# The overflow blocks of a routed expert stage: 32 instead of 33 blocks ahead of the branch

## The chip, the cores and the metric

The kernel runs on one core of a Trainium2 chip. The time is that of the device for one execution, in microseconds (us); smaller is better. The engines are TensorE (PE, with PEld for its weight loads), VectorE (DVE), ScalarE (ACT), GpSimd (POOL) and SyncE (SP), and 16 DMA engines move data between HBM and the on-chip memory.

## The reference

Two blocks of a model run one after the other on 512 tokens of width 1024, in f32. The first block has two layers; each is an attention part, a hierarchical mixture of experts, and a gated embedding. The change touches only the mixture of experts, which runs once in each of the two layers:

```python
expert_id = (g_sel[:, None] * EXPERTS_PER_GROUP + top_i).reshape(-1)   # 2 of 32 experts for each token
counts = jnp.zeros((N_EXPERTS,), jnp.int32).at[expert_id].add(1)
...
def expert_block(args):
    xb, e = args
    hid = jax.nn.silu(xb @ w_gate[e]) * (xb @ w_up[e])
    return hid @ w_down[e]
```

The 512 tokens give 1024 assignments, 32 for an expert in the mean. One expert has three matrices of 1024 x 256, 1024 x 256 and 256 x 1024 in f32, 1 MiB each. The inputs are drawn from a fixed seed, so the counts are the same in every run.

## The kernel before

Each layer runs attention, then merge_and_route (L1375: projections, router, and the tables that say which token sits where), then the experts, then combine_experts (L1914: reads the experts' rows back from HBM, weighs them and adds them to the tokens), then the gate of the embedding.

**The blocks.** The kernel puts assignments into blocks of LANES = 64 rows (L1336). Expert e owns block e, for its first 64 assignments. What an expert has beyond 64 goes to overflow blocks, 32 and up; there can be at most SPILL = 16 of them, so BLOCKS = 48. L1634 to L1647 count them on VectorE: `spills` is the number of overflow blocks of each expert, `ends` its running sum. Three tables come out: r.token (which token each lane gathers; two blocks are one column), r.row (which half row of y_rows each lane scatters to), and r.spill_expert (L1667 to L1670), whose entry j is the expert of overflow block j, at most 31, and whose entry 16 is the number of overflow blocks. For an entry past the last overflow block the value is 31, the cap. An empty lane has an index out of bounds, and the indirect DMA leaves it out.

**experts (L1702)** runs `blocks` blocks from block `first`. Its five engines work as a pipeline:

- SyncE (L1734 to L1751) loads the three matrices of each block into one of U slots, in order. Gate and up of block n wait until block n-U has had its product with gate and up (gu_done), down waits for down_done of block n-U. For a block of 32 or more the expert's number is read from r.spill_expert into a register first (value_load, L1737); nothing in the loads depends on whether the block holds any token. At the end it loads two halves of w_ple, the embedding's weights, into the two gather buffers (L1748).
- GpSimd (L1754) gathers the token rows of a pair of blocks (L1758) and scatters the 64 x 1024 result of each block, as 128 half rows (L1765). At the end it waits for the scatters (L1781).
- TensorE (L1784) turns the rows of a pair (turn, L1789), multiplies with gate and up (L1800), turns the hidden (L1809), multiplies with down (L1818). Block n-1's down runs after block n's gate and up.
- ScalarE applies silu (L1849) and evicts the result (L1844); VectorE scales the turned rows (L1864), multiplies (L1873) and copies (L1879).

It is called in two ways. With `opening`, the call "ex": U is 6 slots, the first 6 blocks' weights and the first 2 pairs' rows were loaded during routing (L1438 to L1445, L1467), and at its end TensorE and ScalarE do the first 4 pieces of the embedding's product (L1835, L1904, L1911). Without it, the call "sp": U is EMBED_SLOT = 3 slots, nothing has been loaded ahead, GpSimd first clears the two gather buffers (L1773), and SyncE waits at its end for the reload of w_ple (L1750), whose place the gathers have taken.

Every such call is a Block: each engine runs its own code, and all five meet at its end. The two calls stand in first_layer:

```python
spilled = nc.values_load(r.spill_expert[0:1, SPILL:SPILL + 1], min_val=0, max_val=SPILL)
experts(k, "ex", r, i, 0, ALWAYS, ...)            # ALWAYS = EXPERTS + 1 = 33
with nc.If(spilled > ALWAYS - EXPERTS):
    experts(k, "sp", r, i, EXPERTS, SPILL, ...)   # 16 blocks from block 32
```

So block 32, the first overflow block, is run by the first call always, and the second call runs all 16 overflow blocks, the first of them again, when there are two or more of them.

Of the kernel before, what the change touches and what calls it, by code (L numbers as in the profile page):

```python
# [75 lines left out]
def sems(k, ctx, names):  # L76

    found = [ctx.enter_context(k.nc.semaphore(n + k.layer)) for n in names.split()]
    assert not k.used_sems & {x.num for x in found}
    k.used_sems |= {x.num for x in found}  # L80
    return found
# [143 lines left out]
def row_piece(w, c, chunks, off, cols):  # L225

    return [(chunks, cols, rows_pc(w)[:, c:c + chunks, off:off + cols])]
# [1106 lines left out]
EXPERTS = GROUPS * PER_GROUP  # L1334
# [1 line left out]
LANES = P // 2  # L1336
SPILL = 2 * S // LANES
BLOCKS = EXPERTS + SPILL
ALWAYS = EXPERTS + 1
SKIP = 65536.0  # L1340


# [352 lines left out]
def expert_parts(k, u, w_gate, w_up, w_down):  # L1695

    gu, down = expert_slot(k, u)
    return [(gu[:, 0, :], w_gate.rearrange("(p c) n -> p (c n)", c=DC)),
            (gu[:, 1, :], w_up.rearrange("(p c) n -> p (c n)", c=DC)), (down, w_down.rearrange("(f p) n -> p f n", p=P))]
# [214 lines left out]
def combine_experts(k, tag, r, y_rows, embedding, st):  # L1914


    nc = k.nc
    rows = y_rows.rearrange("(t p c) d -> p t (c d)", p=P, c=2)
    y = k.expert_ring[:, 0:NT * 2 * D].rearrange("p (t c d) -> p t c d", t=NT, c=2)
    with ExitStack() as ctx:  # L1920
        (*landed, added, multiplied) = sems(k, ctx, " ".join(f"{tag}_landed{t}" for t in range(NT)) + f" {tag}_added {tag}_multiplied")
        block = ctx.enter_context(nc.Block())

        @block.sync
        def _(sp):
            for t in range(NT):
                sp.dma_start(y[:, t, :, :].rearrange("p c d -> p (c d)"), rows[:, t, :]).then_inc(landed[t], 16)
            st.loads(sp, 0, st.RAW)

        @block.gpsimd  # L1930
        def _(pool):
            st.split_highs(pool, 0, st.SPLIT)

        @block.tensor
        def _(pe):
            for i in range(NT, 2 * NT):
                embedding.product(i, k.ps[:, i % NT, :]).then_inc(multiplied, 1)

        @block.scalar
        def _(act):  # L1940
            for i in range(NT, 2 * NT):
                act.wait_ge(multiplied, i - NT + 1)
                embedding.take(i, k.ps[:, i % NT, :])
            act.preload_act_table_set("sqrt_and_others")

        @block.vector
        def _(dve):
            for t in range(NT):
                dve.wait_ge(landed[t], 16)
                for c in (0, 1):  # L1950
                    nc.vector.scalar_tensor_tensor(out=k.x[:, t, :], in0=y[:, t, c, :], scalar=r.gate[:, c, t:t + 1],
                                                   in1=k.x[:, t, :], op0=ALU.mult, op1=ALU.add).then_inc(added, 1)
                    dve.wait_ge(added, 2 * t + c + 1)
# [1195 lines left out]
def first_layer(k, t, i, ctx, following, r, ring_base, scratch, o, line_store):  # L3149


    nc = k.nc
    xn_rows, y_rows = scratch
    st = o.st
    lasting = {x.num for x in st.landed + [st.high_ready, st.low_ready, st.used]}
    ended = k.used_sems - lasting
    early = k.spare[:, 0:6 * S].rearrange("p (j s) -> p j s", j=6)
    route_loads = r.loads(k, ctx, t["w_router_group"][i], t["b_router_group"][i], t["w_router_expert"][i],
                          t["b_router_expert"][i], t["g_ffn"][i])
    k.room(o.branches, "yb_room", [P, 8 * S])  # L3160
    with ExitStack() as room:
        attention, yb_ready, early_ready = differential(
            k, ctx, room, st, [t[n][i] for n in ("lam_q1", "lam_k1", "lam_q2", "lam_k2")], t["g_subln"][i],
            t["c_lam_init"][i], t["c_keep"][i], k.cosT, k.sinT, o.da_raw, o.ybT, early,
            line_store)
    o.branches.close()
    assert -(-nc.sbuf_base // 32) * 32 == ring_base
    mergedT = k.spare.rearrange("p (c s) -> p c s", c=DC)
    m = Merge(k, ctx, "mg", st, MERGE_PIECES, o.packs, ((o.yaT, 4), (o.ybT, 4)), mergedT, o.sig, o.part,
              (0, 1, 2, 3, 4, 7, 5, 6), early, early_ready)  # L3170
    op = Product(k, ctx, "op", st, m.end, DC, mergedT, o.split)
    with ExitStack() as room, ExitStack() as moe:
        k.expert_ring = k.room(room, "expert_ring", [P, RING_SLOTS * EXPERT_WORDS])
        xs = k.room(room, "ex_xs", [P, GATHERS, D])
        embedded = k.spare_tiles
        embedding = Embedding(k, moe, "pe", t["p"][i, 0], t["w_ple"][i], o.rows, embedded)
        embedding.weights_in(xs)
        weights = (t["w_exp_gate"], t["w_exp_up"], t["w_exp_down"])
        expert_loads = Loads(k, moe, *((f"ex_{n}_landed{u}", expert_parts(k, u, *(w[i, u] for w in weights))[part])
                                       for u in range(EXPERT_SLOTS)  # L3180
                                       for n, part in (("gu", slice(0, 2)), ("down", slice(2, 3)))))
        gathered = sems(k, moe, " ".join(f"ex_gathered{u}" for u in range(GATHERS)))
        lasting = {x.num for x in expert_loads.landed + gathered + embedding.loads.landed + [embedding.ready]}
        merge_and_route(k, "rt", st, attention, yb_ready, m, op, r, xn_rows, route_loads, expert_loads, embedding, xs, gathered,
                        ended)
        ended = k.used_sems - lasting
        ctx.close()
        spilled = nc.values_load(r.spill_expert[0:1, SPILL:SPILL + 1], min_val=0, max_val=SPILL)
        experts(k, "ex", r, i, 0, ALWAYS, xn_rows, y_rows, *weights, xs, embedding, (expert_loads, gathered), ended)
        with nc.If(spilled > ALWAYS - EXPERTS):  # L3190
            experts(k, "sp", r, i, EXPERTS, SPILL, xn_rows, y_rows, *weights, xs, embedding)
        before_gate = set(k.used_sems)
        raw = k.expert_ring[:, 2 * NT * D:3 * NT * D].rearrange("p (t d) -> p t d", t=NT)
        gate_stream = Stream(k, following, "pg", [row_piece(t["w_ple_gate"][i], 2 * e, 2, half * 512, 512) for half in (0, 1)
                                            for e in range(4)], raw, ring_base + 4 * 3 * NT * D)
        lasting = k.used_sems - before_gate
        combine_experts(k, "cb", r, y_rows, embedding, gate_stream)
    ended = k.used_sems - lasting

    def ple(ctx, late, sig, junk, following):  # L3200
        return embed_per_layer(k, ctx, "pe", gate_stream, t["g_ple"][i], embedded, sig, junk, late, following, ended), gate_stream

    return ple
# [132 lines left out]
```

## Time and profile before

| | |
|---|---|
| median of 3 runs | 2538.68 us (2536.31 to 2541.02) |
| the profiled execution's own time | 2538.29 us |
| its span (first to last instruction) | 2536.5 us |
| mean granted TensorE clock | 0.966 |
| TensorE busy | 2319.1 us (91%) |
| VectorE, ScalarE, GpSimd busy | 998.9, 586.7, 411.4 us |
| moved by DMA | 402.85 MB, mean 159 GB/s |

A busy time is the sum over one engine's instructions; waits between them are not in it. The span is cut into 40 slices of 63.4 us. The mixture of experts runs from about 482 to 737 us in the first layer and from about 1275 to 1532 us in the second. In the timeline a row has its start, its length, the engine and line, output and inputs, the count of instructions merged into it, and in brackets how long the engine was idle before it and what ended that. SPq is SyncE's issue of a DMA: its length is the issue, not the transfer.

### The profile page before, as it was taken

The numbers are of one execution on the slowest core, as the hardware profiler recorded it, in microseconds if no ns is written. First come the engines' busy times: TensorE is split into PE (matmuls) and PEld (weight loads), VectorE is DVE, ScalarE is ACT, GpSimd is POOL, SyncE is SP. The second block draws the span as 40 slices with busy tenths as digits, with TensorE's granted clock in tenths as the row PEclk, the third lists the DMA queues.
The fourth block names the chain that finished last, engine by engine and source line by source line (L and its number), as shares of the span: only waits on it lengthen the run. The fifth ranks groups of instructions, "written<-read, shape, count | busy, mean of one in ns | idle before, by whom it ended". The sixth has DMA issues, their size and how long they took to land. (4 is left out here: it accounts for less than half of the span.)

```text
span 2536.5 us, 29194 instructions
## 1 busy us (share of the span) xinstructions
PE 2319.1 (91%) x11776; PEld 1707.9 (67%) x11776; DVE 998.9 (39%) x1730; ACT 586.7 (23%) x1211; POOL 411.4 (16%) x404
## 2 busy tenths in 40 slices
PE   7989999698879999999779887899999999999998
PEld 5666788444437766788644445787767887888886
DVE  5445533511125454543521113645553334332234
ACT  2433401211113352420311112423432001200011
POOL 2001121121211101021112211111111211111111
PEclk9999999799989999999889998899999999999999
DMA  4114535799962212233789995222222333233321
GB/s 147 51 50 99 131 105 199 277 414 415 416 253 92 67 34 65 60 91 100 290 342 416 415 367 178 67 83 68 80 84 65 98 96 108 83 93 99 100 91 67
DMA packets 291540, 402.85 MB, mean 159 GB/s; under 512 B 31306, under 2 KB 230730, under 8 KB 273478
## 3 DMA queue, kind: packets, MB, share of 16 engines
q1 hardware_dynamic: 276444, 373.31, 41.7%
q0 software_dynamic: 10176, 16.81, 1.8%
q10 hardware_dynamic: 4778, 10.76, 1.6%
q8 instruction: 98, 1.61, 0.3%
q14 instruction: 44, 0.36, 0.0%
HBM read 388.99 MB, written 30.15 MB: 165 GB/s over the span
## 5 line engine op out<-in xcount | busy, mean ns | idle before, releaser
L136 PE MATMUL banks<-h_split,w_high 128*128 128x512 f32 x2624 | 830.5, 398 | 2.3 <-PEq L3022 1.7
L136 PEld LDWEIGHTS banks<-h_split,w_high 128*128 128x128 f32 x2624 | 482.2, 189 | 108.1 <-issue 8.2
L188 DVE TENSOR_TENSOR w_low<-w_raw,w_high 128x1024 fp32r<-128x1024 f32 (+1 forms) x264 | 316.9, 1202 | 528.4 <-POOL w_high L177 528.4
L177 POOL CAST w_high<-w_raw 128x1024 fp32r<-128x1024 f32 (+1 forms) x264 | 278.4, 1056 | 1474.6 <-PE banks L136 1351.7
L136 PE MATMUL banks<-h_split,w_low 128*128 128x512 f32 x1312 | 515.1, 393 | 0.0
L136 PEld LDWEIGHTS banks<-h_split,w_low 128*128 128x128 f32 x1312 | 246.8, 188 | 55.2
L136 PE MATMUL banks<-w_high,op_split 128*128 128x512 f32 x736 | 231.2, 394 | 0.9 <-DVE mg_part L1264 0.9
L1800 PE MATMUL banks<-expert_ring,ex_xsT 128*64 128x256 f32 x1472 | 176.4, 394 | 12.3 <-DMA expert_ring<-in_w_exp_up 9.3
L136 PEld LDWEIGHTS banks<-w_high,op_split 128*128 128x128 f32 x736 | 138.2, 188 | 34.0 <-DVE mg_part L1264 2.2
L1800 PEld LDWEIGHTS banks<-expert_ring,ex_xsT 128*64 128x64 f32 x1472 | 105.6, 141 | 68.7 <-DMA expert_ring<-in_w_exp_up 10.3
L136 PE MATMUL banks<-w_low,op_split 128*128 128x512 f32 x368 | 144.7, 393 | 0.0
L1765 POOL DMA_INDIRECT y_rows<-ex_y,route_row x66 | 65.8, 997 | 388.8 <-ACT ex_y L1844 388.8
L136 PE MATMUL banks<-w_high,h_split 128*128 128x512 f32 (+1 forms) x384 | 120.0, 387 | 2.7 <-DVE h_split L336 2.5
L1873 DVE TENSOR_TENSOR ex_hid<-ex_silu,banks 128x128 f32<-128x128 f32 x66 | 19.0, 288 | 261.6 <-ACT ex_silu L1849 261.6
L1248 ACT ACTIVATE mg_sig<-banks 128x512 f32<-128x512 f32 x44 | 26.4, 599 | 347.2 <-PE banks L136 347.2
L1818 PE MATMUL banks<-expert_ring,ex_hidT 128*64 128x512 f32 x368 | 96.0, 646 | 0.9 <-issue 0.9
L1789 PE MATMUL banks<-identity,ex_xs 128*128 128x128 f32 x272 | 42.1, 301 | 58.5 <-DMA ex_xs<-xn_rows,route_token 42.2
L136 PE MATMUL banks<-pg_high,h_split 128*128 128x512 f32 x256 | 85.1, 408 | 2.5 <-DVE h_split L336 2.5
L136 PEld LDWEIGHTS banks<-w_high,h_split 128*128 128x128 f32 x384 | 72.0, 192 | 17.9 <-DVE h_split L336 3.7
L1789 PEld LDWEIGHTS banks<-identity,ex_xs 128*128 128x128 f32 x272 | 34.8, 196 | 72.8 <-DMA ex_xs<-xn_rows,route_token 53.6
L1844 ACT ACTIVATE ex_y<-banks 128x512 f32<-128x512 f32 x66 | 39.5, 598 | 189.6 <-PE banks L1818 189.6
L136 PEld LDWEIGHTS banks<-w_low,op_split 128*128 128x128 f32 x368 | 69.1, 188 | 16.0
(422 smaller groups left out, 2782.2 us busy)
## 6 DMA issues: line engine op xcount, KB each, us to landing
w_raw<-in_w_in SPq DMA_DIRECT2D x142, 512.0 KB, 4.1
expert_ring<-in_w_exp_gate SPq DMA_DIRECT2D x46, 1024.0 KB
expert_ring<-in_w_exp_up SPq DMA_DIRECT2D x46, 1024.0 KB
expert_ring<-in_w_exp_down SPq DMA_DIRECT2D x46, 1024.0 KB
w_raw<-in_w_gu SPq DMA_DIRECT2D x44, 512.0 KB, 4.1
region<-in_w_exp_gate SPq DMA_DIRECT2D x20, 1024.0 KB
region<-in_w_exp_up SPq DMA_DIRECT2D x20, 1024.0 KB
region<-in_w_exp_down SPq DMA_DIRECT2D x20, 1024.0 KB
```

Of the source, the lines that this page charges most:

```text
L136: last = nc.tensor.matmul(out, left, right, start=(start and n == 0), stop=(stop and n == 2), skip_group_check=True)
L177: self.nc.gpsimd.tensor_copy(self.high[:, i % self.SPLIT, 0:n], self.raw[:, i % self.RAW, 0:n]).then_inc(self.high_ready, 1)
L188: self.nc.vector.tensor_tensor(self.low[:, i % self.SPLIT, 0:n], self.raw[:, i % self.RAW, 0:n], self.high[:, i % self.SPLIT, 0:n].bitcast ...
L1248: self.nc.scalar.activation(out, gate, ACT.Sigmoid).then_inc(self.sig_done, 1)
L1765: nc.gpsimd.indirect_dma_start(out=y_halves, in_=y[:, n % Y, :], in_offset=None, out_offset=bass.IndirectOffsetOnAxis(ap=r.row[:, at:at + ...
L1789: last = nc.tensor.transpose(k.ps[:, c // 4, (c % 4) * P:(c % 4 + 1) * P], xs[:, q % X, c::DC], k.ident[:])
L1800: last = nc.tensor.matmul(k.ps[LANES * h:LANES * (h + 1), 2 + side, 0:2 * P].rearrange("p (g n) -> p g n", g=2), xsT[:, q % X, c, LANES * ...
L1818: last = nc.tensor.matmul(k.ps[LANES * h:LANES * (h + 1), 5 + n % 2, :], hidT[:, n % 2, LANES * f:LANES * (f + 1)], slots[n % U][1][:, f, ...
L1844: nc.scalar.activation(y[:, n % Y, :], k.ps[:, 5 + n % 2, :], ACT.Copy).then_inc(sem["y_ready"], 1)
L1873: nc.vector.tensor_tensor(hid[:, n % 2, :], silu[:, n % 2, :], k.ps[:, 2 + n % 2, P:2 * P], ALU.mult).then_inc(sem["hid_ready"], 1)
```

## The change

ALWAYS is gone. The first call runs the 32 blocks of the experts, and the branch is taken when there is one overflow block or more; taken, it runs the 16 blocks from block 32, as before.

```diff
-ALWAYS = EXPERTS + 1
...
         spilled = nc.values_load(r.spill_expert[0:1, SPILL:SPILL + 1], min_val=0, max_val=SPILL)
-        experts(k, "ex", r, i, 0, ALWAYS, xn_rows, y_rows, *weights, xs, embedding, (expert_loads, gathered), ended)
-        with nc.If(spilled > ALWAYS - EXPERTS):
+        experts(k, "ex", r, i, 0, EXPERTS, xn_rows, y_rows, *weights, xs, embedding, (expert_loads, gathered), ended)
+        with nc.If(spilled > 0):
             experts(k, "sp", r, i, EXPERTS, SPILL, xn_rows, y_rows, *weights, xs, embedding)
```

## Rows read from the trace of the kernel before

**Rows 1.** The page: the span, and GB/s moved in 40 slices of it.
```profile
span 2536.5 us, 29194 instructions
...
GB/s 147 51 50 99 131 105 199 277 414 415 416 253 92 67 34 65 60 91 100 290 342 416 415 367 178 67 83 68 80 84 65 98 96 108 83 93 99 100 91 67
```

**Rows 2.** A group of the page: out<-in, xcount, busy us, mean ns, idle before.
```profile
L1765 POOL DMA_INDIRECT y_rows<-ex_y,route_row x66 | 65.8, 997 | 388.8 <-ACT ex_y L1844 388.8
```

**Rows 3.** Windows: window, length, busy us (count) by engine, PEclk, DMA share, GB/s.
```profile
600.00:690.00 90.00, 77.00 (x524) 40.07 (x526) 14.71 (x36) 10.26 (x24) 18.26 (x18) 0.95 1.02 416
...
728.10:729.10 1.00, 1.00 (x4) 0.40 (x3) 0.00 (x0) 0.53 (x1) 0.00 (x0) 1.00 0.43 160
730.60:731.60 1.00, 1.00 (x4) 0.41 (x3) 0.00 (x0) 0.48 (x1) 0.00 (x0) 1.00 0.05 5
1526.30:1527.30 1.00, 1.00 (x4) 0.48 (x3) 0.00 (x0) 0.41 (x1) 0.00 (x0) 1.00 0.04 1
737.00:738.00 1.00, 0.00 (x0) 0.00 (x0) 0.00 (x0) 0.00 (x0) 0.00 (x0) 1.00 0.14 41
```

**Rows 4.** DMA view, window 730.6 to 731.6 us.
```profile
DMA packets 80, 0.00 MB, mean 5 GB/s; under 512 B 78, under 2 KB 78, under 8 KB 80
```

**Rows 5.** DMA view, window 1526.3 to 1527.3 us.
```profile
DMA packets 80, 0.00 MB, mean 1 GB/s; under 512 B 80, under 2 KB 80, under 8 KB 80
```

**Rows 6.** Timeline 700 to 745 us: start, length, engine, line, operation.
```profile
704.47 5.36 PE L1800 MATMUL banks<-expert_ring,ex_xsT 128*64 128x256 f32 x32 [2.63 <-DMA expert_ring<-in_w_exp_up]
...
712.98 3.67 PE L1800 MATMUL banks<-expert_ring,ex_xsT 128*64 128x256 f32 x32
...
720.51 3.67 PE L1800 MATMUL banks<-expert_ring,ex_xsT 128*64 128x256 f32 x32 [1.89 <-DMA expert_ring<-in_w_exp_up]
...
728.46 7.13 PE L1904 MATMUL banks<-ex_xs,pe_rows 128*128 128x512 f32 x16
...
729.44 0.98 POOL L1765 DMA_INDIRECT y_rows<-ex_y,route_row  x1 [1.63 <-ACT ex_y L1844]
...
735.63 0.60 ACT L1911 ACTIVATE region<-banks 128x512 f32<-128x512 f32 x1 [1.12 <-PE banks L1904]
...
737.03 2.87 SPq L1927 DMA_DIRECT2D expert_ring<-y_rows  x4
...
740.00 8.54 PE L1904 MATMUL banks<-ex_xs,pe_rows 128*128 128x512 f32 x16 [4.41 <-issue]
```

**Rows 7.** Timeline, the same place of the second layer.
```profile
1508.44 3.67 PE L1800 MATMUL banks<-expert_ring,ex_xsT 128*64 128x256 f32 x32
...
1516.14 3.67 PE L1800 MATMUL banks<-expert_ring,ex_xsT 128*64 128x256 f32 x32 [2.06 <-DMA expert_ring<-in_w_exp_up]
```

**Rows 8.** Timeline of SyncE's DMA issues, first layer, expert loads.
```profile
599.73 4.17 SPq L1742 DMA_DIRECT2D expert_ring<-in_w_exp_gate  x1
...
684.78 3.05 SPq L1742 DMA_DIRECT2D expert_ring<-in_w_exp_gate  x1
...
688.91 4.70 SPq L1744 DMA_DIRECT2D expert_ring<-in_w_exp_down  x1
...
694.41 2.02 SPq L1742 DMA_DIRECT2D expert_ring<-in_w_exp_gate  x1
```

**Rows 9.** Timeline 535 to 575 us, first layer, the pieces of a block.
```profile
541.92 1.00 POOL L1765 DMA_INDIRECT y_rows<-ex_y,route_row  x1 [3.23 <-ACT ex_y L1844]
...
545.57 1.16 PE L1789 MATMUL banks<-identity,ex_xs 128*128 128x128 f32 x8 [0.70 <-DMA ex_xs<-xn_rows,route_token]
...
546.65 1.94 PE L1818 MATMUL banks<-expert_ring,ex_hidT 128*64 128x512 f32 x8
...
568.82 1.00 POOL L1765 DMA_INDIRECT y_rows<-ex_y,route_row  x1 [3.23 <-ACT ex_y L1844]
```

**Rows 10.** Tile view of ex_xs on GpSimd: lengths in ns, min/median/max.
```profile
L1460 POOL MEMSET ex_xs<- x4: 948/952/953, 445.7 to 1240.8; 128x1024 f32 x4
```

**Rows 11.** DMA issues of the page: KB each, median us to landing.
```profile
ex_xs<-xn_rows,route_token POOLq DMA_INDIRECT x34, 8.4
```

## The prediction

> **What bounds the kernel now.** I read the page first, for where memory matters. TensorE is busy for most of the span, yet the change touches only the two expert stages, and there the slices move 414 to 416 GB/s, far more than anywhere else [rows 1]. The windows say more: from 600 to 690 us the DMA share is 1.02 at 416 GB/s, with TensorE busy 77.0 of 90 us [rows 3]. So an expert block is paced by its weights: 3 matrices of 1,048,576 bytes are 3.146 MB, and 3.146 / 415.5 GB/s is 7.57 us. With its gathers and scatters a block takes longer: ten blocks between two issues of a gate matrix, (684.78 - 599.73) / 10 = 8.5 us [rows 8]. TensorE alone could go faster. Early in the stage, when six slots are still full, four blocks pass between two scatters in 568.82 - 541.92 = 26.9 us, 6.73 each [rows 9]. At the end of the stage the reader should see that block 32's first product waits for DMA (1.89 us before 720.51), and block 31's, at 712.98, does not [rows 6].
>
> **Is there an overflow block?** This decides everything, because the branch is entered at one instead of two. All 66 scatters of the trace are 33 blocks in two layers, so the branch was never entered: neither layer has more than one overflow block [rows 2]. What block 32 held can be read from its scatter, the last of each layer. First a gauge: in the us after block 31's scatter in layer 0, 160 KB move, which is 39 rows of 4 KB [rows 3]; the reference's own routing of these inputs, counted, gives expert 31 39 tokens. Block 32 in layer 0 moves 5 KB, and of its 80 packets 78 are under 512 B; the two others are of 2 KB class, and a row is scattered as two halves of 2 KB [rows 3, 4]. So layer 0 has one overflow row. In layer 1 the same scatter moves 1 KB, and all 80 packets are under 512 B: no row [rows 3, 5]. The count of the reference agrees: in layer 0 one expert has 65 tokens, one above the 64 of its block, and in layer 1 the largest has 54. The number of overflow blocks is 1 in layer 0 and 0 in layer 1. With the change the branch is entered in layer 0, for one row, and not in layer 1.
>
> **What goes: block 32 of the first call, in both layers.** Its weights, its half pair's turn (1.16 us), its products. In layer 0 the stage's last gate product starts at 712.98 instead of 720.51: 7.53 us [rows 6]. It could gain a little more: a turn of 1.16 us stood ahead of it [rows 9] and goes, but block 31's matrices land about 7.57 us before block 32's, at 712.9, so I take 7.6. The bounds are 7.5 and 8.7. In layer 1: 1516.14 - 1508.44 = 7.70 [rows 7]. The loads of w_ple are issued behind the last block's weights and move up with them. Behind the last down product the tail is the same (four pieces of embedding, barrier). Sum 15.3 us saved.
>
> **What comes: 16 blocks in layer 0.** The branch has no case for one block; it runs SPILL blocks, each with its 3.146 MB. Blocks 33 to 47 are empty, and their entries of r.spill_expert are all 31, so they load expert 31's matrices fifteen times; nothing skips a load. Step by step, from the moment at which the second call may start:
>
> 1. The first call ends 7.6 us earlier, so SyncE, which issued the next stage's first DMA at 737.03 [rows 6], is at the branch at 729.4.
> 2. It reads the expert's number. Before block 32's gate matrix that made a gap of 694.41 - (688.91 + 4.70) = 0.80 us [rows 8]. First issue at 730.2.
> 3. A first DMA after a pause: y_rows is issued at 737.03 and in the us from 737 41 GB/s move [rows 3, 6], so data flow less than 1 us later. I take 1.0: 731.2.
> 4. The last block's gate and up are in after 15 and two thirds blocks: 15.67 x 7.57 = 118.6 us. Its first product starts at 849.8. No gathers to speak of run beside these loads (one row in all), so I take 7.57, not 8.5.
> 5. The tail. From block 32's gate product to its scatter it was 729.44 - 720.51 = 8.93 us, and the scatter's packets were through by 731.6 [rows 3, 6]: 11.1 us. The embedding's four pieces (7.13 us from 728.46) aren't run again. The barrier: from ScalarE's last end, 735.63 + 0.60, to 737.03 is 0.80 [rows 6]. So the next stage's first issue falls at 849.8 + 11.1 + 0.8 = 861.7.
>
> Against 737.03 that is +124.7 us for layer 0, its saved block already inside.
>
> Is anything else slower than the 7.57? **GpSimd's start:** two memsets of 0.95 us [rows 10], a gather at about 1 us of issue, 8.4 us to landing in the median under load [rows 11], turn and scale: TensorE may start its first product some 6 us after the matrices are in. That is hidden as long as DMA has work, and three free slots are 22.7 us of it. Block 3's down then waits for down_done of block 0, which comes behind block 1's gate product; I work it out to about 27 us after the start, when block 3's gate and up are still arriving (until 27.7). Cover is thin: 0 to 3 us. I take 0. **Three slots instead of six:** from the landing of block n's gate and up to the moment DMA needs down_done of n-1 there are two blocks, 15.1 us; TensorE needs 3.67 for gate and up, 1.16 for a turn and 1.94 for down [rows 6, 9]. Enough. **SyncE:** queued behind each wait for a slot is the read of a register (0.80) and three issues; they run while DMA is two blocks behind. Hidden. **w_ple:** 1.05 MB again, 2.5 us behind the last down matrix, while TensorE is in the 11.1 us tail. Hidden. It would cost its 2.5 us only if the tail were gone.
>
> **The jump.** Before, both layers jumped over the branch's code. TensorE resumed at 740.00, idle 4.41 us, while SyncE issued at 737.03 [rows 6]: 3 us that nobody waited for, since VectorE waited for y_rows. Whether entering the branch costs such a stall the trace can't show. Bounds: below, nothing or a small gain, since layer 0 now runs straight on; above, 4.4 us on SyncE. I take 0, because SyncE's own jump is the nearest row and shows 0.80 with the barrier in it. The Trainium skill (Runtime: NRT & Kernel Launch, section "Instruction fetch mechanics") says that a taken branch to code outside the fetched window stops the engine until that code is in, and calls run-time control flow expensive. By that rule an entered branch could stall SyncE too, and the sum would be about 4 us higher; the trace agrees for TensorE's 4.41 us and not for SyncE's 0.80.
>
> The pace itself: the same skill (DMA: Bandwidth & Descriptors, section "Where 436 GB/s comes from") says that between HBM and the on-chip memory HBM's 358 GB/s per core binds. By it the 16 blocks would take an estimated 19 us more. This trace differs, with its 416 GB/s held over 90 us on one core [rows 3], and the row decides.
>
> **Sum.** +124.7 - 7.7 = +117.0 on the profiled execution's own 2538.29 us, which stands 0.39 us below the median of the three runs: 2655.3 us.
>
> **The rivals.**
>
> - *TensorE paces the branch.* It wakes slowly after a wait for weights: behind 2.63 us idle a gate product took 5.36 instead of 3.67 us [rows 6]. If each block of the branch paid that, TensorE's 6.73 would become 8.42 us and pass DMA's 7.57: 16 x 0.85 = 13.6 us more, 2669. For it: with three slots every block waits a bit. Against it: a wait of 1.89 us still gave 3.67, and the idle time of a block would be 7.57 - 6.73 = 0.84 on the average.
> - *Faster than before: the branch is not entered in layer 0.* The place is the count of overflow blocks in `ends`, the price is 124.7 + 7.6 us, and it turns at one row: with no expert above 64 tokens only the two saved blocks are left, 2538.3 - 15.3 = 2523. For it only that two packets of 2 KB are a thin sign; against it, they are there in layer 0 and not in layer 1, and the reference's count says 65.
> - *Entered in both layers*, if the one row were read wrongly and block 32 held something in layer 1: 2538.3 + 2 x 124.7 = 2788. Rows 5 are against it.
>
> **How the numbers follow.** Forecast 0.84, TensorE's pace 0.11, not entered 0.03, entered twice 0.02. The range: the low end takes the lower pace bound in part (TensorE's 6.73 if reading one expert's matrices over and over let DMA go faster would give 13.6 less, and I give it little) and the larger saving of 8.7: 2645. The high end holds the first rival's 2669, the stall of 4.4 us and the late first slots, 3: 2676. That leaves out the two last rivals, 0.05, and part of the doubt on prices. A change of 0.2%, 5 us, is what a measurement of this kernel can tell from none; no case lies within it. Faster 0.03, slower 0.97.
>
> **What would show each step.** The scatter group has 64 + 16 = 80 instead of 66; DMA moves 16 - 2 = 14 blocks more, 44 MB, about 447 MB in all; the expert slices at 415 GB/s are two longer in layer 0 and none in layer 1. The gap from the last gate product of the branch to y_rows is near 12 us, from SyncE's first load to that product near 120. A pace of 8.4 us with products of 5.36 us would say TensorE; idle SyncE at the entry would say the jump. A scatter count of 64 would make the prediction wrong altogether.

## The result, and the profile after

| | before | after |
|---|---|---|
| median | 2539.85 us (4 runs, 2536.31 to 2544.76) | 2659.25 us (4 runs, 2656.23 to 2662.21) |
| the profiled execution | 2538.29 us | 2656.23 us |
| span | 2536.5 us | 2654.4 us |
| mean granted clock | 0.966 | 0.965 |

The ratio of after to before is 1.0466, with a 95% interval of 1.0449 to 1.0483: the kernel got 4.7% slower. The prediction was 2655.3 us with a range of 2645 to 2676, and the profiled execution stands 0.9 us from it, the median of the four runs 4.0 us above it. The sections below show that this closeness is partly luck: the terms for the first layer's branch fell short by 5 us, and stretches that no term spoke of gave 7.6 back.

The page of the changed kernel, with the lines that answer to [rows 1]:

```profile
span 2654.4 us, 30783 instructions
...
GB/s 142 54 50 110 121 96 254 326 414 415 318 397 379 159 80 40 58 53 88 81 299 345 416 416 274 144 96 80 85 73 56 96 93 111 80 95 97 102 93 67
...
DMA packets 301655, 448.01 MB, mean 169 GB/s; under 512 B 33994, under 2 KB 233418, under 8 KB 280006
```

The slices at more than 300 GB/s go on longer in the first layer, and the bytes are 448.01 MB against 402.85. The difference, 45.2 MB, is 14.4 times 3.146 MB: 16 blocks more, two fewer, and w_ple once more. The view of the scatters' line (columns as in [rows 10]) answers to [rows 2]:

```profile
L1764 POOL DMA_INDIRECT y_rows<-ex_y,route_row x64: 982/992/1020, 499.7 to 1644.2; - x64
...
L1764 POOL DMA_INDIRECT y_rows<-sp_y,route_row x16: 982/992/1023, 755.7 to 863.2; - x16
```

64 scatters of the first call and 16 of the branch, all 16 of them between 755.7 and 863.2 us. So the branch ran once, in the first layer, for the one row beyond an expert's 64, and not in the second. The timeline of the first layer, answering to [rows 6]:

```profile
714.08 3.67 PE L1799 MATMUL banks<-expert_ring,ex_xsT 128*64 128x256 f32 x32 [2.44 <-DMA expert_ring<-in_w_exp_up]
...
729.20 0.60 ACT L1910 ACTIVATE region<-banks 128x512 f32<-128x512 f32 x1 [1.12 <-PE banks L1903]
...
730.93 0.36 SPq L1741 DMA_DIRECT2D expert_ring<-in_w_exp_gate  x1
...
742.48 5.74 PE L1799 MATMUL banks<-expert_ring,sp_xsT 128*64 128x256 f32 x32 [1.47 <-DVE sp_xsT L1863]
...
762.41 3.67 PE L1799 MATMUL banks<-expert_ring,sp_xsT 128*64 128x256 f32 x32 [0.60 <-DMA expert_ring<-in_w_exp_up]
...
854.30 3.67 PE L1799 MATMUL banks<-expert_ring,sp_xsT 128*64 128x256 f32 x32 [1.99 <-DMA expert_ring<-in_w_exp_up]
...
863.22 0.98 POOL L1764 DMA_INDIRECT y_rows<-sp_y,route_row  x1 [1.63 <-ACT sp_y L1843]
...
867.73 2.01 SPq L1926 DMA_DIRECT2D expert_ring<-y_rows  x4
```

Block 31's gate product is now the last of the first call. SyncE's first load of the branch, 730.93, comes 1.1 us after ScalarE's last end (729.20 + 0.60). TensorE starts at 742.48, 11.6 us later, since it needs the gathered rows; from block 35 of the branch (762.41) on it waits for weights; and after the last scatter 4.5 us pass until the next stage's first issue at 867.73. The windows (columns as in [rows 3]) show DMA in the same stretch:

```profile
731.00:732.00 1.00, 0.00 (x0) 0.00 (x0) 0.00 (x0) 0.00 (x0) 0.73 (x2) 1.00 0.29 33
...
732.00:733.00 1.00, 0.00 (x0) 0.00 (x0) 0.00 (x0) 0.00 (x0) 1.00 (x2) 1.00 0.61 172
...
733.00:734.00 1.00, 0.00 (x0) 0.00 (x0) 0.00 (x0) 0.00 (x0) 0.72 (x2) 0.52 0.95 393
...
742.00:848.00 106.00, 93.89 (x634) 51.13 (x636) 17.35 (x43) 11.64 (x27) 18.48 (x19) 0.93 1.02 411
```

After the first issue it takes 2.1 us, to 733, until data flow at nearly the full rate. Then the DMA share is 1.02, as in [rows 3], at 411 GB/s.

Four gate products of the branch, further on in the timeline of TensorE:

```profile
770.12 5.36 PE L1799 MATMUL banks<-expert_ring,sp_xsT 128*64 128x256 f32 x32 [2.06 <-DMA expert_ring<-in_w_exp_up]
...
778.63 3.67 PE L1799 MATMUL banks<-expert_ring,sp_xsT 128*64 128x256 f32 x32
...
785.38 3.67 PE L1799 MATMUL banks<-expert_ring,sp_xsT 128*64 128x256 f32 x32 [1.11 <-DMA expert_ring<-in_w_exp_up]
...
793.08 3.67 PE L1799 MATMUL banks<-expert_ring,sp_xsT 128*64 128x256 f32 x32 [0.81 <-DMA expert_ring<-in_w_exp_up]
```

The first two lie 8.51 us apart, the next 6.75, the next 7.70. One product of four (blocks 36, 40 and 44) runs at half clock, after 2 us of idle, and takes 5.36 us; the block after it then finds its weights in place and waits for nothing. Over 12 blocks, (854.30 - 762.41) / 12 = 7.66 us each.

### The profile page after: what moved, and what is told of

Same layout as the page of the kernel before. It is cut to its first block and busy times, and to the rows that moved or that the text cites. A ratio compares the mean times of both kernels' runs of the same rounds, so it can differ in the third digit from the quotient of the medians.

```text
span 2654.4 us, 30783 instructions
## 1 busy us (share of the span) xinstructions
PE 2407.8 (91%) x12398; PEld 1754.2 (66%) x12398; DVE 1015.9 (38%) x1770; ACT 597.6 (23%) x1239; POOL 434.2 (16%) x426
## 2 busy tenths in 40 slices
DMA packets 301655, 448.01 MB, mean 169 GB/s; under 512 B 33994, under 2 KB 233418, under 8 KB 280006
## 5 line engine op out<-in xcount | busy, mean ns | idle before, releaser
L1799 PE MATMUL banks<-expert_ring,ex_xsT 128*64 128x256 f32 x1408 | 167.5, 392 | 10.9 <-DMA expert_ring<-in_w_exp_up 8.0
L1788 PE MATMUL banks<-identity,ex_xs 128*128 128x128 f32 x320 | 50.1, 304 | 68.9 <-DMA ex_xs<-xn_rows,route_token 52.7
L1788 PEld LDWEIGHTS banks<-identity,ex_xs 128*128 128x128 f32 x320 | 41.4, 197 | 85.9 <-DMA ex_xs<-xn_rows,route_token 64.9
## 6 DMA issues: line engine op xcount, KB each, us to landing
region<-in_w_exp_up SPq DMA_DIRECT2D x20, 1024.0 KB, 20.2
```

Of the source, the lines that this page charges most:

```text
L1788: last = nc.tensor.transpose(k.ps[:, c // 4, (c % 4) * P:(c % 4 + 1) * P], xs[:, q % X, c::DC], k.ident[:])
L1799: last = nc.tensor.matmul(k.ps[LANES * h:LANES * (h + 1), 2 + side, 0:2 * P].rearrange("p (g n) -> p g n", g=2), xsT[:, q % X, c, LANES * ...
```

## The experiments

Theory A is the prediction's: the first call's last block was worth its DMA time, and the branch costs 16 blocks at DMA's pace and a fixed price for entering and leaving. Against it stand: the saved blocks were worth nothing; TensorE paces the branch, by its half-clock products; SyncE's reads of registers or its waits for slots are on the path; the repeated reading of one expert's matrices sets the pace. The traces of the kernels are compared by marks: the first and the last gate product of a call, and the issue of y_rows.

**33 blocks in the first layer, 32 in the second.** This separates the second layer's saved block from everything else.

```diff
-        experts(k, "ex", r, i, 0, ALWAYS, ...)
-        with nc.If(spilled > ALWAYS - EXPERTS):
+        always = ALWAYS if i == 0 else EXPERTS
+        experts(k, "ex", r, i, 0, always, ...)
+        with nc.If(spilled > always - EXPERTS):
```

> The first layer stays as before (33 blocks, branch from two), the second layer runs 32 blocks and enters the branch from one; its count is 0, so it is not entered. My theory: the removed block's weights were on the path, 7.6 to 7.7 us, of which the second layer's stage in the trace after the change shows 5.2 less (y_rows 1532.61 to 1653.73 against its start 1275.38 to 1401.67): the time falls by 5 to 8 us from before, to 2532 to 2535. Rival (the last block was hidden behind other work, and the sum came out for another reason): no change, 2540.

Measured: 2527.75 us against 2539.27 before, ratio 0.995 (0.9927 to 0.9973). It is faster, by 11.5 us in the median (7 to 19 by the interval), where 5 to 8 was expected: the rival of no change is out, and the size was missed. Later it ran again:

> The kernel with 33 blocks in the first layer and 32 in the second, again, with more rounds. The first time it was 11.5 us below before, with an interval from 7 to 19, where the removed block's stage is 8.0 shorter. Theory A (the saving is the block alone): 7 to 9 us below before. Theory B (something else in the kernel before costs 3 to 4 us more): 11 to 12 below.

Measured: 2528.49 us against 2539.22, ratio 0.996 (0.9945 to 0.9975), that is 6 to 14 us below. The second layer's last gate product and y_rows issue in this kernel's timeline:

```profile
1506.12 5.36 PE L1800 MATMUL banks<-expert_ring,ex_xsT 128*64 128x256 f32 x32 [2.30 <-DMA expert_ring<-in_w_exp_up]
...
1524.60 2.57 SPq L1927 DMA_DIRECT2D expert_ring<-y_rows  x4
```

From the layer's first gate product, at 1277.46, to this last one are 228.66 us; in the kernel before it was 1516.14 - 1278.80 = 237.34, and 237.37 in its second trace. So the removed block is worth 8.7 us here up to the last gate product. That product ran at half clock, so 6.7 of them reach y_rows; in the first run of this kernel, where the last product ran at full clock, it is 7.8. The saving is on the path: the rival of "hidden" falls. In the median the 10.7 us lie nearer to theory B's 11 to 12. The rest stands in stretches with the same code: from the first layer's y_rows to the second layer's first gate product 538.4 us pass instead of 541.8 and 540.5 in the two traces of the kernel before, and from the second y_rows to the end 1001.9 instead of 1003.9 and 1004.8. What makes them shorter isn't explained by any row I found.

**33 blocks, and the branch from one overflow block.** This is the price of the branch by itself.

```diff
-        with nc.If(spilled > ALWAYS - EXPERTS):
+        with nc.If(spilled > 0):
```

> Both layers run 33 blocks in the first call, and the branch is entered from one overflow block: entered in the first layer. My theory: after the change plus the two saved blocks, 2659.3 + 12.8 to 15.3 = 2672 to 2675; against before this is the price of the entered branch alone, 132 to 135 us. Rival (the saved blocks were worth nothing): 2659.

Measured: 2677.58 us (2670.27 to 2680.88), ratio to before 1.0538 (1.0507 to 1.0569). The branch costs 138 us with an uncertainty of 8, and the two saved blocks together are 2677.6 - 2659.3 = 18 us by the medians, 2668.1 - 2654.4 = 14 by the spans of the two profiled executions. Both medians lie above the top of what was expected, with intervals that reach into it, and the rival's 2659 is out. The trace is firmer on the branch:

```profile
721.25 3.67 PE L1800 MATMUL banks<-expert_ring,ex_xsT 128*64 128x256 f32 x32 [1.88 <-DMA expert_ring<-in_w_exp_up]
...
874.71 1.99 SPq L1927 DMA_DIRECT2D expert_ring<-y_rows  x4
```

From the last gate product of the first call to y_rows this kernel has 874.71 - 721.25 = 153.5 us, the kernel before 16.5 [rows 6], so the entered branch is 137.0.

**The branch with 4 and with 10 blocks.** The blocks left out are empty here. The second kernel has 10 in place of the 4.

```diff
-            experts(k, "sp", r, i, EXPERTS, SPILL, ...)
+            experts(k, "sp", r, i, EXPERTS, 4, ...)
```

> The changed kernel with 4 instead of 16 blocks in the branch. The 12 blocks left out are empty for these inputs. Theory, DMA paces each at the 7.66 us of the trace: 2659.3 - 91.9 = 2567. Rival 1, TensorE's own pace of 6.73 and a larger fixed price of the branch: 2659.3 - 80.8 = 2578. Rival 2, each block pays a gate product at half clock, 8.42: 2659.3 - 101.0 = 2558.

> The changed kernel with 10 instead of 16 blocks in the branch; the 6 left out are empty for these inputs. Theory (7.66 each): 2659.3 - 46.0 = 2613. Rival 1 (6.73): 2619. Rival 2 (8.42): 2609. With the run of 4 blocks it gives a line whose end at no block is the fixed price of entering: by the trace 867.73 - 729.5 - 16 x 7.66 = 15.7 us.

Measured: 2565.09 us (2562.33 to 2567.92) with 4 and 2611.21 (2610.65 to 2614.51) with 10. The slope from 4 to 16 blocks is (2659.25 - 2565.09) / 12 = 7.85 us a block, from 4 to 10 it is 7.69. The theory's 2567 and 2613 are 2 us off, rival 1 is 13 and 8 off, rival 2 7 and 2. Medians alone don't part 7.66 from 8.42 well at 10 blocks; at 4 they do. The fixed price, from traces: from the first call's last gate product to y_rows, with 4 blocks, 774.49 - 714.44 = 60.1 us; less 16.5 for the way without a branch and 4 x 7.66 it is 12.9. With 16 blocks, 153.65 - 16.5 - 122.6 = 14.6. The difference is in the way out. The kernel with 4 blocks, then the one with 10:

```profile
762.56 3.67 PE L1799 MATMUL banks<-expert_ring,sp_xsT 128*64 128x256 f32 x32 [0.99 <-DMA expert_ring<-in_w_exp_up]
...
771.48 0.98 POOL L1764 DMA_INDIRECT y_rows<-sp_y,route_row  x1 [1.64 <-ACT sp_y L1843]
...
774.49 2.07 SPq L1926 DMA_DIRECT2D expert_ring<-y_rows  x4
```

```profile
817.01 0.98 POOL L1764 DMA_INDIRECT y_rows<-sp_y,route_row  x1 [1.64 <-ACT sp_y L1843]
820.76 1.98 SPq L1926 DMA_DIRECT2D expert_ring<-y_rows  x4
```

With 4 blocks 11.93 us lie between the last gate product and y_rows, as in the prediction's 11.1 + 0.8, and y_rows is issued 3.01 us after the start of the last scatter. With 10 blocks that second distance is 820.76 - 817.01 = 3.75 us, and with 16 it is 4.51, or 4.50, in each of the seven traces with 16 blocks. (From the last gate product it is 13.43 or 13.44 in the five of them where that product ran at full clock.) So it is no chance of one execution: the way out grows by 0.12 to 0.13 us for each block of the branch. What takes this time no row shows, and that 4 blocks meet the prediction's 11.9 is then a coincidence.

**Other experts for the empty blocks.** Blocks 33 to 47 load experts 0 to 14, a fixed number each.

```diff
-                e = b if b < EXPERTS else sp.value_load(r.spill_expert[0:1, b - EXPERTS:b - EXPERTS + 1], ...)
+                e = (b if b < EXPERTS else b - EXPERTS - 1 if b > EXPERTS else
+                     sp.value_load(r.spill_expert[0:1, b - EXPERTS:b - EXPERTS + 1], ...))
```

> The changed kernel, where block 33 and up of the branch load the matrices of experts 0 to 14, a fixed number each, instead of expert 31 fifteen times. These blocks are empty for these inputs. Theory A (the DMA engines pace, whatever is read): the same pace, 7.66 us a block, 2659. Rival B (reading one expert over and over is what makes 7.66 of the 7.57 I used): the pace falls to 7.57, 1.4 us less, which only the trace can show. Rival C (reading it over and over helps): slower than 2659 by more than 5.

Measured: 2655.57 us (2653.52 to 2656.15). From the branch's first to its last gate product 112.09 us, where the changed kernel has 111.82. Theory A holds: whether one expert or fifteen are read makes no difference to the pace. Rivals B and C fall.

**Expert 31 by a fixed number.**

```diff
-                e = b if b < EXPERTS else sp.value_load(r.spill_expert[0:1, b - EXPERTS:b - EXPERTS + 1], ...)
+                e = (b if b < EXPERTS else EXPERTS - 1 if b > EXPERTS else
+                     sp.value_load(r.spill_expert[0:1, b - EXPERTS:b - EXPERTS + 1], ...))
```

> The changed kernel, where block 33 and up load expert 31 by a fixed number: the same bytes, but SyncE reads no register before them. Theory: SyncE's reads (a gap of 0.76 us before each gate issue in the trace) are behind queued loads, so 2659 and the same pace; only the second and third block's first issue come 0.7 us earlier, hidden too. Rival: the reads are on the path, up to 15 x 0.76 = 11 us less, 2648.

Measured: 2654.01 us (2653.18 to 2657.42), and 111.88 us from first to last gate product. The reads of registers are hidden. The median is 5 us lower than the changed kernel's, as with the distinct experts 4 lower; the branch's own length doesn't show it, so it isn't the reads on SyncE's path. About half of it stands elsewhere, in the second layer, where the branch is jumped over. The end of that layer's experts in this kernel:

```profile
1652.68 0.60 ACT L1910 ACTIVATE region<-banks 128x512 f32<-128x512 f32 x1 [1.12 <-PE banks L1903]
1653.74 3.39 SPq L1926 DMA_DIRECT2D expert_ring<-y_rows  x4
```

From ScalarE's last end, 1653.28, to y_rows are 0.46 us, and 0.46 in the kernel of distinct experts too, where the changed kernel has 2.78. That is 2.3 of the 4 and 5 us. The rest isn't explained.

**Four slots instead of three.**

```diff
-    U, X, Y = EXPERT_SLOTS if opening else EMBED_SLOT, GATHERS, 3
+    U, X, Y = EXPERT_SLOTS if opening else RING_SLOTS, GATHERS, 3
```

> The changed kernel with 4 slots of weights in the branch instead of 3. Theory (DMA never idle between 734 and 857 us of the trace): no change, 2659. Rival (waits for a free slot, 69.7 us of SyncE's in the trace, cost something): less than 2655, with a pace under 7.6 us.

Measured: 2658.88 us (2656.15 to 2660.54), 111.71 us from first to last gate product. No change. Here is how such a wait is read; SyncE's longest in the branch of the changed kernel, in the view of waits from 730 to 868 us (total us, times, longest):

```profile
SPq L1743 <- PE banks L1817: 69.7, 13, 8.6
```

69.7 us of waiting for a free slot is the largest row of SyncE's queue, and worth nothing, because the loads issued before it keep the DMA engines at 1.02 all the while.

**Thin loads.** For blocks 33 to 47 one sixteenth of each matrix is loaded; the rest of their weights is left out. What TensorE would do by itself:

```diff
                 gate, up, down = expert_parts(k, n % U, w_gate[layer, e], w_up[layer, e], w_down[layer, e])
+                if b > EXPERTS:
+                    gate, up = ([a[:, 0:128] for a in pair] for pair in (gate, up))
+                    down = [a[:, :, 0:64] for a in down]
```

> The changed kernel, where block 33 and up of the branch load one sixteenth of each matrix; the rest of their weights is left out (these blocks are empty for these inputs). It shows the pace that TensorE would hold by itself. Theory (DMA paces): from 7.66 to about 6.7 us a block, some 14 us less, 2645. Rival (TensorE's half-clock products pace the branch): no more than 3 us less, 2656 or more.

Measured: 2638.26 us (2637.23 to 2647.24), 21 us less than the changed kernel, where 14 was expected. Three gate products in a row, then a window (columns as before):

```profile
791.68 3.67 PE L1802 MATMUL banks<-expert_ring,sp_xsT 128*64 128x256 f32 x32
...
798.50 3.67 PE L1802 MATMUL banks<-expert_ring,sp_xsT 128*64 128x256 f32 x32
...
804.08 3.67 PE L1802 MATMUL banks<-expert_ring,sp_xsT 128*64 128x256 f32 x32
```

```profile
770.00:830.00 60.00, 60.00 (x434) 32.33 (x432) 12.24 (x30) 8.74 (x20) 13.54 (x14) 1.00 0.13 31
```

TensorE is busy all of the 60 us at full clock, and DMA share is 0.13. A pair of blocks takes 6.82 + 5.58 = 12.40 us, 6.20 a block, less than the 6.7 expected. So DMA paces the branch with 7.66, by a margin of 1.46 us, and TensorE's rival falls. The 8.42 of that rival was built on the wrong base too: with the product of every block at half clock, each would take 6.20 + 1.69 = 7.89. That would still be more than DMA's 7.66; the rival falls because only one product of four ran so.

**The kernel before and the kernel after, once more.**

> The kernel before, once more, for a second trace of it. In the first trace 541.77 us lie between the first layer's y_rows issue and the second layer's first gate product, in nine traces of other kernels 537.2 to 539.3, all with the same code there. Theory A (chance of one execution): this trace shows 537 to 540. Theory B (the kernel before is slower there by its own arrangement): 541 to 543 again. The time itself: no change, 2539.

> The changed kernel again, beside the others of this call: 2657 to 2660. From the first layer's y_rows issue to the second layer's first gate product 537 to 539 us. Its last tail in the second layer (20.2 us from the last gate product to y_rows, where the kernel before has 16.5) comes again if it belongs to the arrangement of the code, and is near 16.5 or 18 if it is chance.

Measured: 2537.99 us for the kernel before (12 runs; ratio to its own other runs 0.9999, 0.9988 to 1.0011) and 2657.77 for the changed one, ratio 1.0463 (1.0443 to 1.0483). From the first layer's y_rows to the second layer's first gate product the kernel before has 1279.87 - 739.33 = 540.5 us, after 541.8 in the first trace; the changed one has 538.2, after 537.4. So a difference of 2 to 4 us comes again, but the second trace of the kernel before lies between the two theories: its two traces differ by 1.2 us, so a part of the first trace's 541.8 is chance and the rest goes with the kernel. The tail in the second layer comes again too, 20.18 and 20.20 us in the changed kernel, and 16.47 and 16.46 in the kernel before. It goes with the kernel and is not chance.

## Why the prediction was right, and where it was lucky

Set against the profiled execution, in us, with the same marks:

| step of the prediction | forecast | measured |
|---|---|---|
| start of the first layer's experts | 0 | +1.1 |
| first call one block shorter | -7.6 | -7.5 |
| the branch's first load at (steps 1, 2) | 730.2 | 730.93, or 729.8 without the +1.1 |
| first load to last gate product (steps 3, 4) | 119.6 | 123.4 |
| last gate product to y_rows (step 5) | 11.9 | 13.4 |
| first layer in all, without the +1.1 | +124.7 | +129.6 |
| second layer's stage, first gate product to y_rows | -7.7 | -5.2 |
| y_rows to the second layer's first gate product | 0 | -4.4 |
| from the second y_rows to the end | 0 | -3.2 |
| sum | +117.0 | +117.9 |

**That the branch is entered, and once.** Right, from 2 packets among 80 in [rows 4] against none in [rows 5]. This carried the sign and nearly all of the size. The scatters of the branch and the run without it leave no doubt.

**The saved blocks.** Right: 7.5 us in the first layer. In the second the block itself was worth 8.9 between first and last gate product, and 3.7 of that was given back in the tail (below), so that 5.2 of the forecast's 7.7 reached y_rows.

**Steps 3 and 4.** 3.8 us short. The pace was 7.66 us and not 7.57, which over 15.67 blocks is 1.4. A second part is the way to the full rate: I took 1.0 us from one window of y_rows, in which 41 GB/s moved, and that is when data begin to flow, not when they flow at 400 GB/s, which was at 2.1. By then 0.2 MB had moved, worth 0.5 us, so this part is 0.6. The largest part is one that step 4 left out. It let the last product start when 15 and two thirds blocks were in, as if nothing behind block 47's gate and up moved before them. But the last down matrix was issued at 845.35 and w_ple from 845.78 on, some 8 us before that product, and the window from its start on has:

```profile
854.30:860.00 5.70, 5.65 (x41) 2.92 (x41) 0.30 (x2) 0.54 (x2) 0.00 (x0) 1.00 0.62 243
```

5.70 us at 243 GB/s are 1.39 MB, and after that only the small packets of the two last scatters move. Down and w_ple are 2.10 MB, so 0.7 MB of them had moved ahead of the last product, 1.7 us at 411 GB/s. The three parts are 3.7 of the 3.8 us.

**Step 5.** With 16 blocks 1.5 us more pass than the 11.1 to the last scatter's landing and the 0.8 for the barrier; by the branches of 4 and 10 blocks this grows with the number of blocks, and its cause is open. The second layer's tail, which the prediction took as unchanged, came out longer too:

```profile
1633.55 5.36 PE L1799 MATMUL banks<-expert_ring,ex_xsT 128*64 128x256 f32 x32 [2.36 <-DMA expert_ring<-in_w_exp_up]
...
1650.35 0.60 ACT L1910 ACTIVATE region<-banks 128x512 f32<-128x512 f32 x1 [1.12 <-PE banks L1903]
...
1653.73 2.01 SPq L1926 DMA_DIRECT2D expert_ring<-y_rows  x4
```

The last gate product ran at half clock (+1.7; it took more than 3.67 us in eight of the nine other traces with 32 blocks in the second layer, and in none of the three with 33), and from ScalarE's last end, 1650.95, to y_rows there are 2.78 us, where the kernel before has 0.75 in both its traces. In between, the DMA view of 1650.9 to 1653.7 us lists these queues (packets, MB, share):

```profile
q8 instruction: 1, 0.02, 3.0%
...
q14 instruction: 2, 0.02, 1.5%
```

These are instructions, three packets of them; in the kernel before, nothing moves between its last end and 1532.6. The same three packets stand in this gap in the traces with four slots and with thin loads, where it is 2.81 and 2.85 us. There are none in the kernels in which it is 0.46 (4 blocks, expert 31 by a fixed number, distinct experts), though these jump over the branch's code as well. So the jump cost SyncE about 2 us in some kernels and nothing beyond the barrier in others; no run shows what decides it. The prediction bounded a stall by 0 and 4.4 and took 0, but for entering the branch in the first layer. There 0 was right: SyncE's first load came 1.13 us after ScalarE's last end, with the read of the expert's number in it. For the second layer, which jumps before the change and after it, it had no term. The Trainium skill (Runtime: NRT & Kernel Launch, "Instruction fetch mechanics") says that a jump outside the fetched window waits for a DMA of instructions, and the traces agree where the three packets stand in the gap; the gaps of 0.46 us show the jump without such a wait. For the 1.5 us at the end of the branch in the first layer no instruction packet stands in the gap, and the rule is not shown to be its cause.

**TensorE's pace as a rival.** Its sign was there, products of 5.36 us after 2 us of idle, and its conclusion was wrong: a block that is late by 1.7 us takes it out of the next block's wait as long as TensorE's own 6.20 leaves room. The bound of 6.73 from [rows 9] was itself a pace held up by gathers (0.70 us of idle ahead of a turn), at least in part, so the margin was wider than I thought.

**What no step spoke of.** 7.6 us fewer in stretches whose code is the same. Part of the 4.4 stands at the combining: when the branch was entered TensorE resumes 0.05 us after the y_rows issue, where before it came 2.97 later [rows 6], and the stage is 18.3 instead of 20.2 us long. But entering the branch can't be the whole cause: the kernel that differs from the one before only in the second layer doesn't enter it, and has 538.0 and 538.4 us in its two traces, 3.8 and 3.4 less than the 541.8. The cause stays open.

## What to carry to other kernels

- A branch that is "rarely taken" has a price and a count, and both are read from the trace before it is moved: here one row beyond a capacity of 64 called up 16 blocks, 15 of them empty, whose loads nothing skips, and 137 us were paid where the two saved blocks are worth 14 to 18. For these inputs the version that takes the threshold by layer, 33 blocks where an overflow is there and 32 where none is, beats both kernels, at 2528.5 us.
- Packets under a size in the DMA view tell an empty indirect DMA from one with a single row.
- Where a queue's waits are long, look whether the resource behind it is full. 69.7 us of waits for slots cost nothing, as a fourth slot showed, at a DMA share of 1.02.

## What the runs showed of the hardware that I had not expected

- SyncE's gap between the last work of a stage and its first DMA was the same to 0.01 us in two executions of one kernel (2.78 and 2.79; 0.75 and 0.74), and differed by 2 us between kernels whose code there is the same, with three instruction packets in the gap where it was 2.8 us and none where it was 0.46 or 0.75.
- After the branch, the time from the last scatter to the next stage's first DMA grew with the number of blocks in the branch: 3.01 us with 4, 3.75 with 10, 4.51 with 16, the same to 0.01 us in seven traces.
- TensorE's last product of the first call ended at 729.2 us; from 733 on its granted clock was 0.50, the 1.2 GHz level, and it was back at 1.00, 2.4 GHz, only at 747, some 4.5 us into the first gate product of the branch (742.48). None of it showed in the time, since DMA had three slots of work.
- Reading one expert's 3 MB fifteen times over was neither faster nor slower than fifteen different ones: 111.82 and 112.09 us from the first to the last gate product of the branch.
